# DeltaNet inverse of a fused decoder trunk: 32- and 64-column stationaries for the doubling products, and the second triangle taken by block transposes on VectorE instead of by products

## The reference, cut to what matters

```python
l_mat = jnp.where(strict, jnp.einsum('bhnid,bhnjd->bhnij', k_beta, k) * decay, 0.0)
rhs = jnp.concatenate([v * beta[..., None], k_beta * jnp.exp(g_cum)[..., None]], axis=-1)
sol = lax.linalg.triangular_solve(l_mat, rhs, left_side=True, lower=True, unit_diagonal=True)
```

## Time and profile before

| what | value |
|---|---|
| median of 3 runs | 2998.84 us (2996.97 to 2998.98) |
| the profiled execution, its own time | 3000.31 us |
| its span | 2998.5 us |
| mean granted TensorE clock, share of full speed | 0.982 |
| PE busy | 2896.9 us (97%) |
| PEld busy | 2433.9 us (81%) |
| DVE (VectorE) busy | 1837.0 us (61%) |
| ACT (ScalarE) busy | 1328.9 us (44%) |
| HBM traffic | 164 GB/s over the span |

### The profile page before, as it was taken

The page is one execution under the profiler, slowest core; times in us unless marked ns, Lnnn a source line. Parts: engine busy times, 40 slices in busy tenths (PEclk is TensorE's granted clock), DMA queues, the critical chain, the costliest instruction groups (busy, mean ns, idle before and its releaser), DMA issues.

```text
span 2998.5 us, 37768 instructions
## 1 busy us (share of the span) xinstructions
PE 2896.9 (97%) x14080; PEld 2433.9 (81%) x14080; DVE 1837.0 (61%) x2200; ACT 1328.9 (44%) x1539; POOL 26.4 (1%) x29
## 2 busy tenths in 40 slices
PE   7999999999999999999999999889989999999997
PEld 6888888888887788888888878778778888888886
DVE  5777877877777645555555554556655555555555
ACT  6445454453543444444444444544435444444443
POOL 0000000000000000000000000000000000000000
PEclk9999999999999999999999999899999999999999
DMA  6333443434433345555555545532325555555553
GB/s 268 136 131 121 165 150 125 161 131 144 159 114 112 140 183 194 185 194 192 188 194 182 195 176 185 197 113 96 129 85 199 194 191 187 191 189 194 188 190 112
DMA packets 69411, 493.11 MB, mean 164 GB/s; under 512 B 7712, under 2 KB 8032, under 8 KB 10592
## 3 DMA queue, kind: packets, MB, share of 16 engines
q1 hardware_dynamic: 68112, 487.95, 45.4%
q10 hardware_dynamic: 1232, 4.23, 0.4%
HBM read 490.02 MB, written 2.13 MB: 164 GB/s over the span
## 4 chain that ended last, share of the span: by engine, by line
issue 57%; PE 40%; DVE 1%; ACT 1%; POOL 0%; DMA 0%; POOLq 0%; ACTq 0%; SPq 0%; DVEq 0%
PE ACC L483 12%; PE ACC L485 12%; PE ACC L484 12%; PE SIDE L491 2%; PE SIDE L772 1%; PE SIDE L751 0%; PE ACC L714 0%; PE SIDE L789 0%; PE ACC L715 0%; ACT WORK L1091 0%; PE SIDE L769 0%; DVE W_LO L1132 0%; DMA RAW<-stream 0%; PE SIDE L779 0%; DVE WORK L1477 0%
## 5 line engine op out<-in xcount | busy, mean ns | idle before, releaser
L1132 DVE TENSOR_TENSOR W_LO<-RAW,W_HI 128x1024 fp32r<-128x1024 f32 x912 | 1100.0, 1222 | 722.1 <-ACT W_HI L831 716.8
L831 ACT ACTIVATE W_HI<-RAW 128x1024 fp32r<-128x1024 f32 x912 | 961.5, 1059 | 1260.9 <-PE ACC L485 1249.6
L483 PE MATMUL ACC<-W_HI,X_HI 128*128 128x512 f32 x2496 | 992.1, 397 | 15.3 <-DVE W_LO L1132 13.3
L485 PE MATMUL ACC<-W_HI,X_LO 128*128 128x512 f32 x2496 | 975.2, 391 | 0.0
L484 PE MATMUL ACC<-W_LO,X_HI 128*128 128x512 f32 x2496 | 973.7, 390 | 0.0
L483 PEld LDWEIGHTS ACC<-W_HI,X_HI 128*128 128x128 f32 x2496 | 471.1, 189 | 108.8 <-issue 14.0
L485 PEld LDWEIGHTS ACC<-W_HI,X_LO 128*128 128x128 f32 x2496 | 469.8, 188 | 100.3
L484 PEld LDWEIGHTS ACC<-W_LO,X_HI 128*128 128x128 f32 x2496 | 471.0, 189 | 92.6 <-issue 0.6
L483 PE MATMUL ACC<-W_HI,A_HI 128*128 128x512 f32 x1088 | 433.6, 398 | 12.9 <-issue 12.9
L485 PE MATMUL ACC<-W_HI,A_LO 128*128 128x512 f32 x1088 | 426.8, 392 | 0.0
L484 PE MATMUL ACC<-W_LO,A_HI 128*128 128x512 f32 x1088 | 426.3, 392 | 0.0
(11 more groups left out here) (216 smaller groups left out, 1584.2 us busy)
## 6 DMA issues: line engine op xcount, KB each, us to landing
RAW<-stream SPq DMA_DIRECT2D x456, 1024.0 KB, 4.8
WORK<-gdn_rows ACTq DMA_DIRECT2D x8, 512.0 KB, 3.6
WORK<-xt SPq DMA_DIRECT2D x4, 512.0 KB, 9.4
H<-x SPq DMA_DIRECT2D x2, 1024.0 KB, 17.8
out<-WORK SPq DMA_DIRECT2D x4, 512.0 KB, 3.9
WORK<-tails SPq DMA_DIRECT2D x2, 512.0 KB, 12.7
WORK<-gfin SPq DMA_DIRECT2D x1, 1024.0 KB, 6.7
K<-consts SPq DMA_DIRECT2D x1, 678.0 KB, 16.2
```

What stands on the lines that cost most here:

```text
L483: nc.tensor.matmul(dst, hi[:, at:at + P], wh, start=first and h % 2 == 0 and q == 0, stop=False)
L485: m = nc.tensor.matmul(dst, lo[:, at:at + P], wh, start=False, stop=last and h % 2 == 1 and q == 1)
L831: nc.scalar.activation(W_HI[:, h % WS, :], raw_piece(h), ACT.Copy).then_inc(hi_ready, 1)
L1132: nc.vector.tensor_tensor(W_LO[:, h % WS, :], raw_piece(h), W_HI[:, h % WS, :].bitcast(f32), SUB).then_inc(lo_ready, 1)
```

## The change

Levels 0 to 3 (blocks up to 32) stay inside the four 32x32 diagonal blocks of a unit, so the stationary operand is cut to these. YB now holds N's diagonal blocks, masked for each of the four levels (made once per group on VectorE in the new step `masks`). UQ holds the diagonal blocks of the transpose, YQ is block diagonal. `y` and `t` are then 8 matmuls with 32-column stationaries and 128 moving columns (`quad_products`), which write 32 partitions. Levels 4 and 5 use stationaries of 64 columns and 64 moving columns (`block_products`). The `u` products are gone. Instead VectorE transposes TR in 32x32 blocks into UF (whole for levels 0 to 3; 2 and 4 blocks per unit for levels 4 and 5), and ScalarE copies what the next `t` needs into UQ, UB or UR. All take-outs of `y`, and those of `t` at levels 4 and 5, are now copies on ScalarE, for levels 0 to 3 four copies of 32 partitions. `t` at levels 0 to 3 is four subtractions of 32x128 on VectorE.

```diff
+        def quad_products(p, lhs, rhs):
+            for u in range(8):
+                m = nc.tensor.matmul(SIDE[p][0:32, u * P:(u + 1) * P], lhs[:, u * 32:(u + 1) * 32],
+                                     rhs[:, u * P:(u + 1) * P], **ONE)
+            m.then_inc(side_full[p], 1)
+        def block_products(p, lv, lhs, rhs):
+            for u in range(8):
+                a, b = lhs(u), rhs[:, u * P:(u + 1) * P]
+                dst = SIDE[p][0:64, u * P:u * P + 64]
...
             elif kind == "t":
                 gdn_done(pe, f"y{lv}", it)
-                unit_products(p, UR, Y_OF[lv])
-            elif kind == "u":
-                unit_products(p, Y_OF[lv], UR)
+                pe.wait_ge(u_ready, g * STEP_UPS + (lv + 1))
+                if lv < QUADS:
+                    quad_products(p, UQ, YQ)
...
             elif name == "nr":
                 act.wait_ge(n_ready, g + 1)
-                nc.scalar.activation(NR[:, :], N, ACT.Copy).then_inc(n_hi, 1)
+                for r in range(4):
+                    i = nc.scalar.activation(units(NQ[:, :], 32)[32 * r:32 * r + 32, :, :], quad(N, r), ACT.Copy)
+                i.then_inc(nc_done, 1)
...
-            elif name == "y4":
+            elif kind == "y":
                 act.wait_ge(side_full[p], n)
...
+                if lv < QUADS:
+                    for r in range(4):
+                        i = nc.scalar.activation(quad(YQ[:, :], r), quad(SIDE[p][:, :], 0, r), ACT.Copy)
...
+            elif kind == "u":
+                act.wait_ge(u_turned, g * LEVELS + (lv + 1))
+                if lv < QUADS - 1:
+                    for r in range(4):
+                        i = nc.scalar.activation(units(UQ[:, :], 32)[32 * r:32 * r + 32, :, :], quad(UF, r), ACT.Copy)
+                elif lv == QUADS - 1:
+                    nc.scalar.activation(UB[:, :].rearrange("p (u a n) -> p u a n", a=2, n=32), odd(units(UF)), ACT.Copy)
+                    i = nc.scalar.activation(UR[:, :], UF, ACT.Copy)
...
-            elif kind == "y" and lv < MASKED:
+            elif kind == "t" and lv < QUADS:
                 dve.wait_ge(side_full[p], n)
-                nc.vector.tensor_tensor(units(YR[:, :]), units(side[:, :]), every(K_LV + lv * P), MUL)\
-                  .then_inc(side_out[p], 1)
-            elif kind in ("t", "u"):
...
+                for r in range(4):
...
+                    i = nc.vector.tensor_tensor(part, part.bitcast(f32), w_, SUB)
+                i.then_inc(side_out[p], 1)
+            elif kind == "u":
+                gdn_done(dve, f"t{lv}", it)
+                t_ = TR[:, :].bitcast(f32)
+                if lv < QUADS:
+                    i = nc.vector.transpose(UF, t_)
```

More of the change, by code:

```diff
@@ L146 @@
     17 v1
-    18 o
-    19 osum
-    24 oscale
+    19 o
+    20 osum
+    25 oscale
     31 o_t""")
@@ L169 @@
     17 v1
-    18 o
-    19 osum oscale
-    21 o_t""")
+    18 o osum
+    19 oscale
+    29 o_t""")
 PREP_STEPS = gdn_table(PREP, """
-    0 factors
-    8 qk_t
-    8 dif
+    1 factors
+    8 qk_t dif
     9 conv_qk0a
     11 conv_qk0b
-    13 conv_qk1a
-    15 conv_qk1b
+    14 conv_qk1a conv_qk1b
     16 silu_qk squares
     17 ss
[L183 to L188, removed]
+    18 decay qkn beta
+    19 v_t
+    22 k_t kkqk
+    23 nr init
+    27 masks""")
 FIRST_STEPS = gdn_table(ONCE, """
@@ L197 @@
     15 fill factors qkn
-    17 k_t v_t
-    17 dif decay beta
-    18 kkqk nr init""")
+    17 k_t v_t dif decay beta
+    18 kkqk nr init masks""")
 def gdn_steps(it, hs):
@@ L538, in unit_products @@
             m.then_inc(side_full[p], 1)
+        def quad_products(p, lhs, rhs):
[7 more added lines that the diff above has]
+                dst = SIDE[p][0:64, u * P:u * P + 64]
+                if lv == QUADS:
+                    b = b.rearrange("p (a two n) -> p a two n", two=2, n=32)[:, :, 0, :]
+                    dst = dst.rearrange("p (a n) -> p a n", n=32)
+                else:
+                    b = b[:, 0:64]
+                m = nc.tensor.matmul(dst, a, b, **ONE)
+            m.then_inc(side_full[p], 1)
         def gdn_step_tensor(pe, name, p, g, it):
@@ L924, in gdn_step_scalar @@
             elif name == "fill":
[L925 to L927 removed]
+                nc.scalar.activation(units(TR[:, :])[:, :, 1::2], every(K_ID)[:, :, 1::2], ACT.Copy).then_inc(tu_fill, 1)
             elif name == "factors":
@@ L1664, in _ @@
             dve.memset(cin[:, :, 0:3], 0.0)
[L1665 to L1666 removed]
+            dve.memset(YQ[:, :].bitcast(f32), 0.0).then_inc(pad_zero, 1)
             dve.wait_ge(pad_zero, 1)
@@ L1725, in constants @@
     K[:, K_M1T:K_M1T + P] = -1.0 * couples(i, i[:, None], 1)
-    for lv in range(MASKED):
-        K[:, K_LV + lv * P:K_LV + (lv + 1) * P] = couples(i[:, None], i, 2 << lv)
+    for lv in range(QUADS):
+        K[:, K_LV + lv * 32:K_LV + (lv + 1) * 32] = couples(i[None, :32], i[:, None] % 32, 2 << lv)
+    K[:, K_I32:K_I32 + 32] = i[:, None] % 32 == i[:32]
+    K[:, K_C1:K_C1 + 32] = -1.0 * couples(i[None, :32], i[:, None] % 32, 1)
     FAR = 1e33
```

104 lines of the change are left out of this document (74 added, 30 removed).

## The result

| | before | after |
|---|---|---|
| median | 2998.75 us | 3007.6 us (3004.42 to 3015.49) |
| the profiled execution, its own time | 3000.31 us | 3009.79 us |
| its span | 2998.5 us | 3008.0 us |
| mean granted TensorE clock | 0.982 | 0.978 |

The ratio of after to before is 1.0035, with a 95% interval of 1.0023 to 1.0046. The kernel became 0.35% slower. The forecast of 3001 us was 6.6 us too low, the range held, and "slower" had a chance of 0.34. The ring that was forecast is there, 8.92 us a level for 8.86. Taken too low was the cost of the clock behind `t4`, and a small wait before `ru` was missed.

What follows compares the result with a forecast made beforehand. TensorE bounded the kernel; the change would turn its gain into waits on ScalarE and VectorE. 8.8 - 8.2 = 0.6 us per solve saves 5, the clock costs 7: 3002.3 us profiled, median 3001, range 2966 to 3035.

Steps and rivals of the forecast that it cites:

- The ring: On ScalarE and VectorE, from one `t` to the next: operations one behind the other sum to 8.86 us per level.
- 8.8 us per solve: TensorE's own work per solve falls by 5.0 (`u` groups) + 2.4 (32-column groups) + 1.4 (64x64 groups).
- the rival of narrow stationaries without gain: TensorE's narrow stationaries give no shorter matmuls: 12 us more, 3013 us; chance 0.14.
- Four subtractions 1.20: VectorE's four 32x128 subtractions in each level's ring take 1.20 us, at 0.30 each.
- Transpose 1.22 + 0.08: VectorE's 128x1024 transpose in the ring takes 1.22 us, with two hand-overs 0.08; bounds 0.6 and 2.3.
- The rival of the slow transpose: VectorE's transpose takes 2.3 us instead of 1.22, the ring 9.9, and the kernel ends at 3036 us; chance 0.15.
- The waits sum to 8.2: TensorE's waits before `t1` to `t4` sum to 7.5 to 8.4 us per solve, taken as 8.2.
- The ring to `t4`: UB and UR copies, `silu_v` and two copies replace the eight: 8.9 us in all, a wait of about 2.2.
- The clock, 8 x 0.5 x 1.7 = 7 us: Behind the wait before `t4`, half of the solves have one 3.4 us stretch at half speed, costing 1.7 us.
- Other edits at zero: `fill`, `nr` and `masks` in turns 15 to 27, and the moved `o`, `osum` and `oscale`, cost zero.
- The sum: Whole kernel: 3000.31 - 5 + 7 = 3002.3 us for a profiled execution, so a median of 3001 us.
- The signs: Profile after: iteration 119 to 121 us; wrong if no idle before `t1` to `t4`, or waits elsewhere, as before `nw`.

Runs made afterwards that it cites:

- e4: Changed kernel with 128-column stationaries again in the y and t groups of levels 0 to 3, plus two small VectorE copies in `masks`; 3007.46 us, ratio 1.0041.
- e1: Changed kernel with ScalarE rounding the weight piece before the inverse's step instead of behind it, turns 0 to 11 of iterations 1 to 8; 2964.08 us, ratio 0.9896.
- e3: Changed kernel with the whole block transpose of levels 0 to 3 done twice on VectorE; 3045.98 us, ratio 1.0159.
- e10: Changed kernel with, at levels 0 to 2, four 32x256 transposes of the diagonal blocks and one 128x256 UQ copy; 2987.54 us, ratio 0.9960.
- e8: Changed kernel with only tables edited: `qk_t` in turn 9 and SIDE0, `silu_v`, `u4`, `conv_qk0a` and `conv_qk0b` in later turns; 3000.42 us, ratio 1.0008.
- e6: Changed kernel with the rounding first of e1 and the tables of e8 together; 2949.16 us, ratio 0.9832.
- e2: Changed kernel with nine more 512-column matmuls into SIDE1 before `t4`; 3012.71 us, ratio 1.0059.

## Why the prediction was right or wrong, point by point

- *TensorE is the bound now, and the change takes 8.8 us per solve from it.* Right; 9.1 by the account above. The 32-column groups took 0.060 for each matmul, below the 0.067 taken and near the lower end of the stream; so the f32 cases of the earlier trace rows were no guide, and the rival of narrow stationaries without gain fell. e4 also shows that its price of 12 us was too high: with 128-column stationaries in the eight groups of levels 0 to 3 the median is the same. The 81 ns of the Trainium skill, page "TensorE: Matmul & The Clock Gate", section "Back-to-back issue gap", fit neither form of this kernel: 105 ns with 128 columns, 60 with 32.
- *A ring of 8.86 us per level on ScalarE and VectorE.* Right: 8.92. The largest error of a single term is 0.12, the UQ copies (1.72 for 1.60), of which the other terms take back half. e1, e3 and e10 each changed one link or its place and moved the level by what the ring says, to 7.49, 10.19 and 8.11; e4 changed TensorE's groups, and the level stayed at 8.91.
- *Four subtractions 1.20; by the rule of the Trainium skill, page "VectorE: DVE Perf Modes", section "Two Vector instructions with no wait between them", 1.36.* They took 1.18 to the transpose. The trace agrees with the rule: the four operations last 277 ns in the mean and 1.15 together, so they are 0.29 apart and none overlaps the next, where the four 128-partition ones in the earlier trace rows do. What was off is the length, 0.28 and not the 0.34 used for the estimate.
- *Transpose 1.22 + 0.08.* Right, 1.28. The rival of the slow transpose fell, and e3 shows what it would have done.
- *The waits sum to 8.2.* 8.21, and here the fit is in part luck. The ring to `t4` left out `qk_t` on both engines. Its matmuls give TensorE 0.85 us more to do between `y4` and `t4` (605.54 to 606.39), so YB alone, ready at 610.8, would have made `t4` wait about 1.4 us and not 2.2. Its take-out, which frees SIDE1, adds 1.25 (610.80 to 612.05), and the wait is 2.68. The rows of before, had this take-out right behind the copies of `y4` (602.99, L836). The 1.31 before `t1` came out near the low end of its 1.1 to 2.0, and that made up for the 0.5.
- *The clock, 8 x 0.5 x 1.7 = 7 us.* This is the term that was mis-sized. In the full iterations the clock fell in every solve and cost 3.06 us, 12 us in four of them where this term gave 3.4. The place was right (behind `t4`, where no wait hides it), and e8 shows the other half of the argument, half speed inside the ring at no cost. Two things were taken too low, each by about two: how often it comes, and how long it lasts (6.8 us behind a wait of 2.68, where the earlier trace rows have 3.40 behind 1.41). Outside the full iterations the term was nearer: the first two solves have 3.4 us each behind `t3`, inside the ring, and the seventh 3.4 us behind `t4`. The prediction also said that before has no stretch at 0.50 between 100 and 1000 us; its own show two, and two more start at 175.61 and 878.76.
- *Other edits at zero.* Nearly right for the turns named, wrong for one place not looked at: `ru` waits 0.50 us per solve. VectorE's four block transposes of level 5 (1.78 us) stand before `conv_qk0b` and the W_LO ahead of `nw`'s take-out; in e8 and e1, where TensorE comes there earlier, the wait is 1.21 and 1.14, and in e6 with `conv_qk0b` moved it is gone.
- *The sum.* Per full iteration the forecast was -0.6 + 0.9 = +0.3; it was +2.84. Of the 2.5 between them 2.2 are the clock and 0.5 `ru`, less 0.3 of TensorE's own work.
- *The signs.* An iteration of 122.85 us lies outside the 119 to 121 that were named, and the wait before `ru` is one of those "elsewhere" by which the prediction called itself wrong. What held is the ring; the total stayed in the range because the range was wide and the clock's excess came in only four of the eight solves.

The last two solves got shorter by 1.4 us in all. In the seventh (0.35) the half speed behind `t4` stands in for one of equal length that before had from 878.76, so this solve lost nothing more to the clock. For the eighth (1.05) no such account was made. Left open is also what decides in which wait of a solve the half speed sets in and how long it lasts. After, e2, e4, e8 and e10 differ in it, and the runs only show where it is.

## What to carry to other kernels

When a change takes work from the bound engine and puts small operations on two others, add up the way round the dependence, operation by operation in queue order, before looking at any share of busy time; with 48 and 61% busy, ScalarE and VectorE bounded this kernel for 36 of the 123 us of an iteration (`t0` to `t4`). Then ask of each queue what stands ahead of the awaited operation without being awaited itself: moving the weight rounding in front of the copies gave 43 us (some 3 of 7 us per iteration by the clock), and a few lines of tables another 15 by the medians, 19 by the ratios. Count the buffer that an operation writes as one of its operands, and price a wait by what follows it too.
